# First inputs by tiles, two weights in halves, and products that start column by column, in a fused two-block transformer kernel

## The reference

```
# first block, twice (l = 0, 1): x = x + hybrid_layer(x)
h = rmsnorm(x, norm_g)                 # x * rsqrt(mean(x*x) + eps) * norm_g
p = h @ w_in                           # 1024 -> 3488, split into 15 sections
cq, ckv, kr, g_a, ..., mq, mk, mv, g_d = split(p)
q = rmsnorm(cq) @ mla_w_uq ; kv = rmsnorm(ckv) @ mla_w_ukv   # latent attention
o_a = attention ; o_b = gated short convolution ; o_c = spatial gate ; o_d = attention
y = concat(o_a*silu(g_a), ..., o_d*silu(g_d)) @ w_out

# second block, twice: adaptive shift and scale, attention, layer norm,
# then a mixture of 32 experts with top-2 routing, layer norm
mod = silu(c) @ ada_w[i] + ada_b[i]    # 1024 -> 6144
y = sum over experts of (silu(h @ w_gate) * (h @ w_up)) @ w_down
```

## Time and profile before

| what | value |
|---|---|
| median of 3 runs | 1566.41 us (1564.67 to 1573.24) |
| the profiled execution, its time | 1563.89 us |
| the profiled execution, its span from the first to the last instruction | 1562.2 us |
| mean granted TensorE clock | 0.949 of full speed |
| PE busy | 1389.6 us (89%) |
| DVE busy | 571.8 us (37%) |
| ACT busy | 215.0 us (14%) |
| DMA over the span | 533.32 MB, mean 341 GB/s |

### The profile page before, as it was taken

One profiled execution on the slowest core, in us unless ns is written; L12 is line 12 of the kernel. 1 busy time (PEld: TensorE's weight loads), 2 busy tenths in 40 slices (PEclk: granted clock), 3 DMA queues, 4 the chain that ended last, 5 costly groups with the idle time before them and its releaser, 6 DMA issues.

```text
span 1562.2 us, 28408 instructions
## 1 busy us (share of the span) xinstructions
PE 1389.6 (89%) x12800; PEld 883.6 (57%) x12800; DVE 571.8 (37%) x1254; ACT 215.0 (14%) x574; POOL 88.4 (6%) x95
## 2 busy tenths in 40 slices
PE   7999999999998999779879788878999797897795
PEld 4885478578886556346446344457655453463451
DVE  3696469655745111101101115684222011011013
ACT  2230123022332000000000002442100000000000
POOL 3100111000003000000000001100200000000000
PEclk9999999999999999889899898999999998998997
DMA  9656845768768999999999998257999999999995
GB/s 345 216 197 233 291 164 198 275 220 288 280 278 340 411 426 426 428 426 426 427 426 428 427 376 320 89 201 282 374 413 426 428 426 427 427 426 427 425 415 201
DMA packets 96856, 533.32 MB, mean 341 GB/s; under 512 B 5184, under 2 KB 7424, under 8 KB 73168
## 3 DMA queue, kind: packets, MB, share of 16 engines
q1 hardware_dynamic: 92992, 519.40, 82.6%
q0 software_dynamic: 3728, 11.95, 2.2%
HBM read 530.28 MB, written 1.05 MB: 340 GB/s over the span
## 4 chain that ended last, share of the span: by engine, by line
PE 65%; DMA 24%; DVE 4%; SPq 4%; ACT 1%; issue 1%; DVEq 0%; ACTq 0%
PE bk L433 28%; PE bk L898 16%; DMA ring<-in_moe_w_down 15%; DMA AR<-in_moe_w_down 9%; PE bk L932 8%; PE bk L614 4%; PE bk L942 4%; SPq L2325 3%; PE bk L429 3%; DVE AR L1017 2%; PE bk L643 1%; PE bk L658 1%; ACT AR L1831 1%; DMA ring<-in_w_in 1%; DVE AR L1025 0%
## 5 line engine op out<-in xcount | busy, mean ns | idle before, releaser
L898 PE MATMUL bk<-ring,AR 128*32 128x128 f32 x4480 | 268.6, 409 | 0.1
L1017 DVE TENSOR_TENSOR AR<-bk,AR 128x128 f32<-128x128 f32 (+2 forms) x106 | 41.3, 390 | 521.6 <-ACT AR L1831 455.6
L898 PE MATMUL bk<-AR 128*32 128x128 f32 x3712 | 223.0, 409 | 0.0
L898 PEld LDWEIGHTS bk<-ring,AR 128*32 128x32 f32 x4480 | 175.7, 127 | 80.9 <-DVE X L1017 4.5
L433 PE MATMUL bk<-ring,AR 128*128 128x256 f32 (+2 forms) x736 | 214.1, 449 | 6.3 <-ACT AR L1831 2.6
L932 PE MATMUL bk<-ring,AR 128*32 128x512 f32 x608 | 159.4, 704 | 51.9 <-DMA ring<-in_moe_w_down 51.1
L1831 ACT ACTIVATE AR<-bk 128x512 f32<-128x512 f32 (+4 forms) x178 | 72.1, 422 | 948.2 <-PE bk L898 774.1
L898 PEld LDWEIGHTS bk<-AR 128*32 128x32 f32 x3712 | 145.5, 127 | 68.5 <-DVE X L1017 4.5
L433 PEld LDWEIGHTS bk<-ring,AR 128*128 128x128 f32 x736 | 140.9, 194 | 73.7 <-issue 56.6
L932 PE MATMUL bk<-AR 128*32 128x512 f32 x416 | 150.9, 709 | 27.8 <-DMA AR<-in_moe_w_down 27.8
L433 PE MATMUL bk<-AR,ring 128*128 128x256 f32 (+1 forms) x832 | 170.5, 364 | 1.7 <-DVE AR L1022 1.4
(11 more groups left out here) (152 smaller groups left out, 954.1 us busy)
## 6 DMA issues: line engine op xcount, KB each, us to landing
ring<-in_moe_w_gate SPq DMA_DIRECT2D x36, 2048.0 KB, 28.6
ring<-in_moe_w_up SPq DMA_DIRECT2D x34, 2048.0 KB, 25.0
ring<-in_moe_w_down SPq DMA_DIRECT2D x34, 2048.0 KB, 33.6
AR<-in_moe_w_up SPq DMA_DIRECT2D x30, 2048.0 KB, 29.9
AR<-in_moe_w_gate SPq DMA_DIRECT2D x28, 2048.0 KB, 26.3
ring<-in_ada_w SPq DMA_DIRECT2D x24, 2048.0 KB, 11.0
AR<-in_moe_w_down SPq DMA_DIRECT2D x22, 2048.0 KB, 33.6
ring<-in_w_in SPq DMA_DIRECT2D x12, 2048.0 KB, 12.6
```

The source lines that it names most:

```text
L898: ins = eng.matmul(o[32 * f:32 * f + 32, 128 * m:128 * m + 128], XG[u][:, c, 32 * j:32 * j + 32], w[:, c, f::4], start=c == 0, stop=c == N ...
L1017: return eng.tensor_tensor(o, a, b, op)
```

## The change

It has five edits, all in the two layers of the first block and the head of the program.

1. SP starts X in two loads, one for each tile of 128 tokens, and in another order: tile 0, identity, tile 1, `norm_g`. Each has its own semaphore, and each reader waits for what it reads.
2. In layer 0 PE turns all eight columns of tile 0, into four banks, and then all eight of tile 1 (`first_columns`).
3. The weights `cq` and `qk` of layer 0 are each loaded by two DMAs: columns c = 0 to 3 with a semaphore of their own, and c = 4 to 7 with the slot's.
4. `chunk` (for `cq` and `qk` in both layers) waits column by column: before the matmul of column c for the half of the weight that holds it (layer 0) and for the bank of columns that holds it.
5. On ACT, in both layers, the even columns go first and the squares of X behind them. On DVE in layer 1, `extract` goes ahead of the wait for `xsq`.

```diff
+        HALVES = ("in", 0, "cq"), ("in", 0, "qk")
...
+            def turn_column(src, o, t, c):
+                a = src[:, t, :].rearrange("p (k c) -> p c k", c=NC)[:, c, :]
+                return turn(o[:, c % 2 * 256 + t * 128:c % 2 * 256 + t * 128 + 128], a)
+
+
+            def first_columns():
+                pe.wait_ge(sem("ident"), 16)
+                pe.wait_ge(sem("x0"), 16)
+                o = [begin(b, "xT", 0, b) for b in range(4)]
+                for c in range(NC):
+                    turn_column(X, o[c // 2], 0, c)
+                pe.wait_ge(sem("x1"), 16)
+                for c in range(NC):
+                    ins = turn_column(X, o[c // 2], 1, c)
+                    if c % 2:
+                        end(ins, "xT", 0, c // 2)
...
                     o = begin(b, "in", l, seg, t)
-                    pe.wait_ge(*loaded("in", l, seg))
-                    wait_columns("xT", l)
                     w = piece(("in", l, seg), NC, n)
-                    end(product(o[:, 0:n], [(HT[:, c, t * 128:(t + 1) * 128], w[:, c, :]) for c in range(NC)]),
-                        "in", l, seg, t)
+                    for c in range(NC):
+                        if ("in", l, seg) in HALVES and c < NC // 2:
+                            pe.wait_ge(sem(f"half_{seg}"), 16)
+                        else:
+                            pe.wait_ge(*loaded("in", l, seg))
+                        pe.wait_ge(*drained("xT", l, c // 2))
+                        ins = eng.matmul(o[:, 0:n], HT[:, c, t * 128:(t + 1) * 128], w[:, c, :], start=c == 0, stop=c == NC - 1)
+                    end(ins, "in", l, seg, t)
...
                 if l:
                     pe.wait_ge(*drained("out", l - 1, 1, 1))
+                    columns(X, "xT", l)
                 else:
-                    pe.wait_ge(sem("x"), 48)
-                columns(X, "xT", l)
+                    first_columns()
...
+                v.wait_ge(sem("ng"), 16)
                 for b in (1, 3):
...
+                if l:
+                    extract(next(n_tot))
                 v.wait_ge(sem("xsq"), l + 1)
...
                 if not l:
                     rope_tables()
                 else:
-                    extract(next(n_tot))
                     ada(8)
...
                 if l:
                     s.wait_ge(*drained("out", l - 1, 1, 1))
                 else:
-                    s.wait_ge(sem("x"), 48)
+                    s.wait_ge(sem("ng"), 16)
+                even_columns("xT", l, ng[:, l])
+                if not l:
+                    s.wait_ge(sem("x0"), 16)
+                    s.wait_ge(sem("x1"), 16)
                 for t in range(NT):
                     ins = act(JUNK, X[:, t, :], ACT.Square, accum_out=st[:, 32 + t:33 + t])
...
-                even_columns("xT", l, ng[:, l])
...
+                if name in HALVES:
+                    h = dst.shape[1] // 2
+                    eng.dma_start(dst[:, 0:h, :], src[:, 0:h, :]).then_inc(sem(f"half_{name[2]}"), 16)
+                    dst, src = dst[:, h:2 * h, :], src[:, h:2 * h, :]
                 eng.dma_start(dst, src).then_inc(sem(f"slot{s}"), 16)
...
-            eng.dma_start(cst[:, 0:K_S1], A["cst"][:, 0:K_S1]).then_inc(sem("x"), 16)
-            eng.dma_start(ng[:, :, :], A["norm_g"]).then_inc(sem("x"), 16)
-            eng.dma_start(X[:, :, :], A["x"].rearrange("(t p) d -> p t d", p=P)).then_inc(sem("x"), 16)
+            eng.dma_start(X[:, 0, :], A["x"][0:P, :]).then_inc(sem("x0"), 16)
+            eng.dma_start(cst[:, 0:K_S1], A["cst"][:, 0:K_S1]).then_inc(sem("ident"), 16)
+            eng.dma_start(X[:, 1, :], A["x"][P:2 * P, :]).then_inc(sem("x1"), 16)
+            eng.dma_start(ng[:, :, :], A["norm_g"]).then_inc(sem("ng"), 16)
```

More of the change, by code:

```diff
@@ L440, in columns @@
                         for t in range(NT):
-                            a = src[:, t, :].rearrange("p (k c) -> p c k", c=NC)[:, 2 * b + ci, :]
-                            ins = turn(o[:, ci * 256 + t * 128:ci * 256 + t * 128 + 128], a)
+                            ins = turn_column(src, o, t, 2 * b + ci)
                     end(ins, tag, i, b)
+            def turn_column(src, o, t, c):
[12 more added lines that the diff above has]
+                        end(ins, "xT", 0, c // 2)
             def wait_columns(tag, i):
@@ L1036, in rope_tables @@
                 v.wait_ge(sem("in"), 80)
-                v.wait_ge(sem("x"), 48)
                 v.step(eng.tensor_copy(posf[:, :], posi[:, :]))
@@ L1173, in spatial_shifts @@
                     v.wait_ge(sem("in2"), 16 * (8 + DEPTH))
-                    v.wait_ge(sem("x"), 48)
+                    v.wait_ge(sem("ident"), 16)
                     v.tell(tt(SGD, bcast(ident, 1, 4), bcast(sgb[:, l, :], 2, 128), ALU.mult), sem("sgd"), l + 1)
```

## The result

| what | before | after |
|---|---|---|
| median of 20 runs | 1566.34 us (1560.3 to 1573.24) | 1563.08 us (1555.93 to 1566.66) |
| ratio of the times | | 0.9973, 95% interval 0.996 to 0.9986 |
| the profiled execution, its time | 1563.89 us | 1559.44 us |
| its span | 1562.2 us | 1557.7 us |
| mean granted clock | 0.949 | 0.954 |

0.9973 of 1566.34 is 4.2 us less, and the interval reaches from 2.2 to 6.3 us. The forecast had 6.7 us. So the time (1563.08) lies 3.4 us above the forecast of 1559.7 and inside the range, and it is within 0.5% of before, as the larger chance said. The forecast sum of 6.7 us lies above that interval, and the traces say which terms were too large.

The account below looks back on a forecast made before the run. PE's chain was taken to bound the kernel, with weight loads setting the first expert stage; 3.1 (first product) + 1.9 (border gap) + 1.7 (border clock) = 6.7 us, giving 1559.7 us, range 1555.5 to 1566.

Parts of the forecast that it names:

- The first product in layer 0: Head of layer 0: first `cq` matmul at 9.4 instead of 12.52 us, 3.1 us gained, bounds 0.9 and 3.7.
- all data behind it moves up by 0.91 us: Program head: X's tile 0 issued at 0.81 instead of 1.72 us, so all later loads come 0.91 us earlier.
- The rule of the Trainium skill, "DMA: Bandwidth & Descriptors", Bandwidth: Loads at the start: two 512 KB DMAs take 0.7 us more than one of 1 MB; the sum becomes 6.0 us.
- The pattern stays: Layer 0 clock: transposes, gap, products, some 3 us at half level as before; 0 gained, bounds 1.7 either way.
- The border: Start of layer 1: PE goes on right behind its transposes, 1.9 us, and the clock does not fall, 1.7 us.
- the clock falls all the same: Rival at the border to layer 1: the clock still falls there; sum 5.0 us, 1561.4 us; chance 0.2.
- the rule that the prediction took from the Trainium skill, "TensorE: Matmul & The Clock Gate", Part 4: Border: transposes do not count as PE work for the clock, so it still falls; sum 5.0 us.
- Who is late next: Both layers: later squares stay hidden, DVE's 1.85 us wait for `ada` is covered by 3.35 us idle; no cost.
- The slower rival: Layer 0: first `ada` weight lands later, costing PE from 8.2 us of lateness; at the extreme 1569.7 us; chance 0.06.
- halves land together: Rival in layer 0: both halves of `cq` land at the same time; sum 4.5 us, 1561.9 us; chance 0.12.
- the first expert product 6 to 7 us earlier: Sign expected at the first expert stage: its first product comes 6 to 7 us earlier than before.
- the prediction's last sign of being wrong: Before the expert stage: the prediction is wrong if the gain is there at 200 us and gone at 490.

Follow-up runs that it names:

- cq_whole: Kernel after, but weights `cq` and `qk` of layer 0 each in one load again; one run, 1559.71 us.
- x_whole: Kernel after, but X in one DMA as the first load and no second wait in the transposes; 1562.08 us, ratio 0.9969.
- x_table: Kernel after, with X in one first load and a tiny activation ahead of ACT's first wait, loading its table early; one run, 1557.0 us.
- best: Kernel after, with X in one load, ACT's table loaded early and POOL's `finish` released only behind DVE's gate multiplications; 1555.67 us, ratio 0.993.
- warm: Kernel after with 12 small dummy matmuls on PE before, between and behind the first runs of transposes; 1560.85 us, ratio 0.9967.
- delay: Kernel after with the `cq` tile 0 products of layer 1 issued five times, 22.2 us more on PE; 1585.95 us, ratio 1.0132.
- order_alone: Kernel before with, in layer 1 alone, ACT's columns ahead of its squares; PE still waits for all four banks; one run, 1562.4 us.

## Why the prediction was right in sign and too large in size

**The first product in layer 0 (3.1 us forecast, 2.0 measured).** The half weight gave what it was to give: the first half lands 2.1 us ahead of the second (10.4 and 12.5). What failed is "all data behind it moves up by 0.91 us": the second half lands at 12.5, where the whole weight landed before. `cq_whole` says the same with the halves away (12.90). With two half loads of X and the small identity load between them, X's second tile came 0.5 us later than the whole X did, and the rate from 4 to 5 us fell to 174 GB/s. The weight was issued at 2.66 instead of 2.19, behind one more issue of SP, and the prediction gave that issue no cost because the queue was full; at a DMA share of 0.74 it was not. `x_whole` has X 1.6 us earlier than the kernel after (5.8 and 7.4). It changes three things at once, so the small load behind the first, the size of the first two and the issue saved (the weight goes out at 2.28) were not told apart. The rule of the Trainium skill, "DMA: Bandwidth & Descriptors", Bandwidth, had the right sign here: by it most of the head start was gone. (The straight line between its two figures gives 0.6 us, where the prediction rounded to 0.7.)

**"The pattern stays", clock in layer 0 (0 forecast, 1.7 lost on average).** This is the step that failed most. For the pair of profiled executions it held (20.0 and 19.97 us for the 48 instructions), but by luck: the trace of before happened to be the one of four old heads whose clock fell again. The time of the 48 instructions shows the clock:

| head | traces | first product | 48 instructions | first `rsb` sum, mean |
|---|---|---|---|---|
| as before | 4 | 12.51 to 12.56 | 18.31 three times, 20.0 once | 31.10 |
| X in two tiles, halves | 4 | 10.54 to 10.66 | 19.97, 20.36, 20.43, 21.08 | 30.89 |
| X whole (`x_whole`, `x_table`, `best`) | 3 | 9.73 to 10.90 | 18.28 to 18.66 | 28.48 |
| two tiles with PE's pauses filled (`warm`) | 1 | 10.74 | 18.31 | 28.89 |

The prediction had read the half level at 14 to 17 us in the one trace of before and taken it for the pattern; it was the one of four in which the clock, at full by the first product, fell again. In the changed head the first products are at the half level each time, also in `cq_whole` (19.90), because the clock comes up late: its first entry is at 14.0 to 16.2 us in the five traces, at 10.2 to 11.3 in the four old heads. So 1.9 us of earlier start become 0.2 us by the `rsb` sums. These are means of four and four, so the 0.2 is loose: against the three old heads whose clock stayed up (30.7) the new one is 0.2 us later, against the fourth (32.4) 1.5 earlier. What goes with the late rise is the pause within the transposes: eight, 0.54 to 1.30 us of nothing, eight. Transposes in one run bring the clock up by 9.9 to 11.3 us, also with the same 1.08 us gap behind them (`x_whole`), and filling the pauses by 6.5. The traces for it are few, five with the pause and eight without, and no run takes away the pause alone: `x_whole` also starts its transposes 1.3 us later, `warm` also fills the time ahead of them and behind them.

**The border (1.9 + 1.7 = 3.6 us forecast, 3.9 measured).** From the first transpose of layer 1 to the products near 420 us it is 261.6 us in the three traces with the old border and 257.7 (without the 22.3 of `delay`) in the nine with the new one, 258.9 with the order of ACT alone (2.6 of the 2.9 us expected). The gap was gone, as the forecast had it. The clock fell in 3 of 3 old borders and in 0 of 10 others. The rival *the clock falls all the same* is ruled out, and this case does not bear out the rule that the prediction took from the Trainium skill, "TensorE: Matmul & The Clock Gate", Part 4, as far as it was applied here: by it PE would have been idle from 159.6 to 162.4 us, and the clock stood at 1.00 all through. The start says it too: in the four old heads PE runs nothing but transposes ahead of its first product, and that product starts at full-level steps, 0.35 us (in the kernel before until 13.7 us).

**Who is late next.** Nothing new held PE, as worked out. DVE waited 1.92 us for the `ada` weight (1.85 forecast), and 1.34 us of the 3.35 us of idle time were left when it emptied `q`. The match of 1.92 and 1.85 is luck: DVE stood there at 32.7 and not at 31.55, and the weight came 1.1 us late as well. The squares stay hidden: ACT empties `cq` tile 0 at 22.40, still held by POOL, and PE has no gap there. In layer 1 ACT was held to 168.07 by PE's products, not by POOL's root. The slower rival did not come up: the `ada` weight landed at 34.5 us, 1.1 later than the 33.4 worked out, where 8.2 were needed. The rival *halves land together* is ruled out by 10.4 and 12.5.

**The sum.** 0.2 + 3.9 = 4.1 us, and the runs measured 4.2 (2.2 to 6.3); with the 0.2 as loose as it is, so close an agreement is chance. Had the head kept its 2.0 us, 2.0 + 3.9 would have been near the forecast. The forecast "the first expert product 6 to 7 us earlier" was wrong in the profiled execution (0.6 us), and by the prediction's last sign of being wrong (a gain that is there at 200 us and gone at 490) nearly so. The two reasons differ from execution to execution: the clock, which fell near 420 us in 8 of 13 traces but not in the one of before, and the meeting of DVE and POOL. `delay` shows that a shift itself is kept. One trace could not have sized the change.

## What to carry to other kernels

Start a product at its first operand, column by column, where PE would else wait for the last copy: a gap closed on PE can also save a fall of the clock, here as much again. Splitting an input to start sooner can cost it back: the last piece came later, and with a pause between two short runs of transposes the clock came up later, 14.0 to 16.2 us instead of 10.2 to 11.3. Before calling a clock pattern fixed, look at more than one execution; and look at what an engine off the path does to DVE at the moment when PE waits for DVE.

## What the runs showed of the hardware that was not expected

- The clock column can read 1.00 while the steps are at the half level: 11 to 14 us after the change, with weight loads 0.69 us apart. Ahead of the first entry in the record of the clock (14.0 us here) the step tells more than the column.
- Transposes alone brought TensorE's clock to the full level: in the four traces with the old head the first entry is at 10.2 to 11.3 us, with nothing but 16 transposes run on PE from 7.0 on.
- Two DVE multiplications of 128x128 took from 0.48 to 4.70 us, by where they fell against POOL's additions of 128x1024. Started 0.7 us ahead of the additions they took 0.96 us (`order_alone`, first stage) and 0.6 us behind them 4.22.
- A load of 1 MB that is first in the queue was there 5.0 us after its issue (5.8), and two of 512 KB with 64 KB between them took 6.6 us from the first issue to the last landing (0.81 to 7.4).
- ACT's table load, 1.28 us, stands behind the wait of the first activation. As long as the squares of X came first it cost nothing; with the copies first it lies on the way to the first product once X is early, and one tiny activation ahead of the wait moved it to 0.80 us.
